# First norm of a two-block layer: x turned raw into place, the root spread by TensorE, two units fed tile by tile

## What is computed

```python
def rms_norm(x, w):
    xf = x.astype(jnp.float32)
    y = xf * lax.rsqrt(jnp.mean(xf * xf, axis=-1, keepdims=True) + RMS_EPS)
    return (y * w.astype(jnp.float32)).astype(x.dtype)

h = rms_norm(x, norm_mix[i])
proj = h @ w_in          # 3*1024 columns q, k, v, 1024 z, then 8 b and 8 a (the gates)
beta = jax.nn.sigmoid(b)
g = -jnp.exp(a_log) * jax.nn.softplus(a + dt_bias)
...
x = x + y                # raw x is needed again after the mixer
```

## Time and profile before

| | |
|---|---|
| median of 3 executions | 1184.47 us |
| the profiled execution | 1184.73 us |
| its span | 1182.8 us |
| TensorE busy | 1120.5 us (95%) |
| VectorE, ScalarE, GpSimd busy | 591.1, 468.8, 486.8 us |
| DMA | 100.36 MB, 85 GB/s on average |

### The profile page before, as it was taken

One profiled execution on the slowest core, in us unless ns is written; L12 is line 12 of the kernel. 1 busy time (PEld: TensorE's weight loads), 2 busy tenths in 40 slices (PEclk: granted clock), 3 DMA queues, 4 the chain that ended last, 5 costly groups with the idle time before them and its releaser, 6 DMA issues. The chain is left out here.

```text
span 1182.8 us, 16417 instructions
## 1 busy us (share of the span) xinstructions
PE 1120.5 (95%) x5820; PEld 908.8 (77%) x5820; DVE 591.1 (50%) x1246; ACT 468.8 (40%) x1002; POOL 486.8 (41%) x280
## 2 busy tenths in 40 slices
PE   5998989999999899999999999989999999999995
PEld 4887778888887787887888888867788887656674
DVE  3696835556655564632122125445754654344465
ACT  5544235555544342342232243243334434343343
POOL 4576312223225495585475475445121211123230
PEclk9999999999999899999999999989999999999998
DMA  7443332211112432632642643503102020001011
GB/s 218 124 111 98 108 83 67 63 46 48 52 36 73 151 111 86 196 122 75 195 133 62 196 144 106 156 20 87 47 26 81 1 63 19 19 9 37 19 37 71
DMA packets 161174, 100.36 MB, mean 85 GB/s; under 512 B 24064, under 2 KB 154444, under 8 KB 160076
## 3 DMA queue, kind: packets, MB, share of 16 engines
q1 hardware_dynamic: 160812, 98.80, 28.7%
q10 hardware_dynamic: 288, 0.59, 0.1%
HBM read 96.21 MB, written 3.16 MB: 84 GB/s over the span
## 5 line engine op out<-in xcount | busy, mean ns | idle before, releaser
L1160 POOL TENSOR_TENSOR wlo<-stage,whi 128x1024 fp32r<-128x1024 f32 (+1 forms) x105 | 272.5, 2599 | 261.9 <-ACT whi L705 261.8
L2092 PE MATMUL ps<-hhi,whi 128*128 128x512 f32 (+1 forms) x744 | 308.2, 414 | 13.8 <-DVE zs L1445 5.5
L2092 PE MATMUL ps<-hlo,whi 128*128 128x512 f32 (+1 forms) x744 | 303.8, 408 | 0.0
L2092 PE MATMUL ps<-hhi,wlo 128*128 128x512 f32 (+1 forms) x744 | 296.8, 399 | 0.0
L2092 PEld LDWEIGHTS ps<-hhi,whi 128*128 128x128 f32 (+1 forms) x744 | 142.1, 191 | 57.6 <-issue 17.1
L2092 PEld LDWEIGHTS ps<-hhi,wlo 128*128 128x128 f32 (+1 forms) x744 | 142.0, 191 | 25.7
L705 ACT ACTIVATE whi<-stage 128x1024 fp32r<-128x1024 f32 x104 | 109.5, 1055 | 130.8 <-PE ps L2092 99.8
L2092 PEld LDWEIGHTS ps<-hlo,whi 128*128 128x128 f32 (+1 forms) x744 | 142.3, 191 | 24.5 <-issue 3.1
L1249 POOL TENSOR_TENSOR wlo<-stage,whi 128x1024 fp32r<-128x1024 f32 (+3 forms) x40 | 73.4, 1838 | 197.3 <-ACT whi L990 197.3
L2092 PE MATMUL ps<-ahi,whi 128*128 128x512 f32 x320 | 127.6, 399 | 5.0 <-POOL alo L1237 3.3
L1066 ACT ACTIVATE prob<-ps,aneg 128x128 f32<-128x128 f32 (+1 forms) x96 | 50.6, 527 | 201.4 <-issue 103.8
(11 more groups left out here) (365 smaller groups left out, 1804.5 us busy)
## 6 DMA issues: line engine op xcount, KB each, us to landing
stage<-dn_w_in SPq DMA_DIRECT2D x32, 512.0 KB, 4.0
stage<-mlp_w_up SPq DMA_DIRECT2D x32, 512.0 KB, 4.5
stage<-mlp_w_down SPq DMA_DIRECT2D x32, 512.0 KB, 4.6
mod_w<-ada_w SPq DMA_DIRECT2D x8, 1536.0 KB, 6.5
stage<-w_in SPq DMA_DIRECT2D x17, 512.0 KB, 3.6
gcrow<-gc_rows SPq DMA_DIRECT2D x16, 256.0 KB, 3.3
stage<-dn_w_out SPq DMA_DIRECT2D x8, 512.0 KB, 3.6
stage<-w_in SPq DMA_DIRECT2D x9, 256.0 KB, 3.1
```

What stands on the lines that cost most here:

```text
L1160: pool.tensor_tensor(wlo[:, slot, 0:ks, 0:cols], stage[:, slot, 0:ks, 0:cols], whi[:, slot, 0:ks, 0:cols], ALU.subtract).then_inc(s["w_lo" ...
L2092: mm = pe.matmul(bank, w[:, slot, k - ks[0], 0:width], x[:, k], start=(i == 0), stop=(i == len(todo) - 1))
```

## The change

The gain is loaded as 8 rows of 128 (4 KB) and turned by TensorE into a column `gcol`. TensorE turns raw x of each token tile as soon as it has landed, in two PSUM banks, and VectorE copies 1024 columns at once into `xT`, its place for later. The reciprocal root of a token tile becomes a diagonal matrix (`tensor_scalar` of the identity), and a product of ones by that diagonal gives a row of roots on all partitions (`ps` bank 1), copied to `rsrow` by ScalarE. Then VectorE makes eight normed tiles `hf0` from `xT`, `gcol` and `rsrow`, all in SBUF, where x had been; ScalarE copies each to `hhi`. The low parts are made by VectorE (even tiles, after all eight) and GpSimd (odd tiles, between its second and third weight split). TensorE feeds the gate unit and the first key unit together: all of high by high, tile by tile as they come; then low weights by high; then high weights by low. The key weights' high part is now made ahead of the tiles. The raw turns and their copies between the later units are gone. The squares of ScalarE go to `hlo` rather than PSUM.

```diff
@@ -320,8 +320,12 @@
-        gbc = sb("gbc", [P, D])
-        xr = sb("xr", [P, 2, D])
+        rsrow = sb("rsrow", [P, T])
+        diag = sb("diag", [P, CH, P])
+        ones0 = sb("ones0", [P, P])
+        nmix = sb("nmix", [P, P])
+        gcol = sb("gcol", [P, KT])
+        hf0 = at("hf0", [P, KT, T], F32, act_at)
...
@@ -705,21 +709,22 @@
...
-            act.dma_start(gbc[:, :], A["norm_mix"].broadcast_to([P, D])).then_inc(s["gbc_in"], 16)
+            act.dma_start(nmix[0:KT, :], A["norm_mix"][0].rearrange("(k p) -> k p", p=P)).then_inc(s["nm_in"], 16)
...
-                act.activation(ps[:, 6:8, :], xn[:, c, :].rearrange("p (b n) -> p b n", b=2), ACT.Square,
+                act.activation(hlo[:, KT - 2:KT, :], xn[:, c, :].rearrange("p (b n) -> p b n", b=2), ACT.Square,
                                scale=float(D) ** -0.5, accum_out=msq[:, c:c + 1]).then_inc(s["x_sq"], 1)
...
-            for f in range(2 * CH):
-                c, half = f // 2, f % 2
-                act.wait_ge(s["h_tr"], f + 1)
...
-            for n in range(1, 4):
+            act.wait_ge(s["rs_ps"], CH)
+            act.activation(rsrow[:, :], ps[:, 1, :], ACT.Copy).then_inc(s["rs_ev"], 1)
+            split_hi(1, 1)
+            for k in range(KT):
+                act.wait_ge(s["x_f"], k + 1)
+                act.activation(hhi[:, k], hf0[:, k], ACT.Copy).then_inc(s["h_hi"], 1)
+            for n in range(2, 4):
                 split_hi(n, n)
...
@@ -781,10 +786,6 @@
...
-                if h == 1:
-                    for k in range(6, KT):
-                        act.wait_ge(s["xtr"], k + 1)
-                        act.activation(xT[:, k], ps[:, (2, 3, 6, 7)[k - 4], :], ACT.Copy).then_inc(s["xev_a"], 1)
...
@@ -1161,6 +1162,7 @@
...
+            pool.memset(ones0[:, :], 1.0).then_inc(s["ones_set"], 1)
...
@@ -1170,8 +1172,13 @@
...
             pool.tensor_copy(whi[:, 0, :, 0:BA_N], stage[:, 0, :, 0:BA_N]).then_inc(s["ba_hi"], 1)
-            for n in range(4):
-                split_lo(n, n, BA_N if n == 0 else P)
+            split_lo(0, 0, BA_N)
+            split_lo(1, 1)
+            for k in range(1, KT, 2):
+                pool.wait_ge(s["h_hi"], k + 1)
+                pool.tensor_tensor(hlo[:, k], hf0[:, k], hhi[:, k], ALU.subtract).then_inc(s["h_lo_p"], 1)
+            for n in range(2, 4):
+                split_lo(n, n)
...
@@ -1327,30 +1334,26 @@
...
-            def x_normed(c):
-                if c >= 2:
-                    dve.wait_ge(s["h_tr"], (c - 1) * 2)
...
+            dve.wait_ge(s["nm_tr"], 1)
+            dve.tensor_copy(gcol[:, :], ps[:, 0, 0:KT]).then_inc(s["nm_col"], 1)
+            for c in range(CH):
                 dve.wait_ge(s["x_rms"], c + 1)
                 dve.reciprocal(rtok[:, 1, c:c + 1], rtok[:, 0, c:c + 1]).then_inc(s["x_inv"], 1)
                 dve.wait_ge(s["x_inv"], c + 1)
-                dve.scalar_tensor_tensor(out=xr[:, c % 2], in0=xn[:, c, :], scalar=rtok[:, 1, c:c + 1], in1=gbc[:, :],
-                                         op0=ALU.mult, op1=ALU.mult).then_inc(s["x_nrm"], 1)
+                dve.tensor_scalar(diag[:, c, :], K["ident"], rtok[:, 1, c:c + 1], None, ALU.mult).then_inc(s["x_dg"], 1)
+                b = 2 + c % 3 * 2
+                dve.wait_ge(s["xtr"], c + 1)
+                dve.tensor_copy(xT[:, :, c * P:(c + 1) * P], ps[:, b:b + 2, :].rearrange("p b (k i) -> p (b k) i", k=KT // 2))\
+                    .then_inc(s["xev"], 1)
+            dve.wait_ge(s["nm_col"], 1)
+            dve.wait_ge(s["xev"], CH)
+            dve.wait_ge(s["rs_ev"], 1)
+            for k in range(KT):
+                dve.scalar_tensor_tensor(out=hf0[:, k], in0=xT[:, k], scalar=gcol[:, k:k + 1], in1=rsrow[:, :],
+                                         op0=ALU.mult, op1=ALU.mult).then_inc(s["x_f"], 1)
+            for k in range(0, KT, 2):
+                dve.wait_ge(s["h_hi"], k + 1)
+                dve.tensor_tensor(hlo[:, k], hf0[:, k], hhi[:, k], ALU.subtract).then_inc(s["h_lo"], 1)
...
@@ -1422,9 +1425,6 @@
...
-            for k in range(6):
-                dve.wait_ge(s["xtr"], k + 1)
-                dve.tensor_copy(xT[:, k], ps[:, (2, 3, 6, 7)[k % 4], :]).then_inc(s["xev_d"], 1)
...
@@ -2100,43 +2100,60 @@
...
-            for f in range(2 * CH):
-                c, half = f // 2, f % 2
...
+            pe.wait_ge(s["nm_in"], 16)
+            pe.transpose(ps[:, 0, 0:KT], nmix[0:KT, :], ident[0:KT, 0:KT]).then_inc(s["nm_tr"], 1)
+
+            def raw_turn(c):
+                pe.wait_ge(x_in[c], 16)
+                if c >= 3:
+                    pe.wait_ge(s["xev"], c - 2)
+                for k in range(KT):
+                    mm = pe.transpose(ps[:, 2 + c % 3 * 2 + k // 4, k % 4 * P:(k % 4 + 1) * P], xn[:, c, k * P:(k + 1) * P], ident)
                 mm.then_inc(s["xtr"], 1)
+
+            def root_row(c):
+                pe.wait_ge(s["x_dg"], c + 1)
+                pe.matmul(ps[:, 1, c * P:(c + 1) * P], ones0[:, :], diag[:, c, :], start=True, stop=True).then_inc(s["rs_ps"], 1)
+
+            pe.wait_ge(s["ones_set"], 1)
+            raw_turn(0)
+            for c in range(1, CH):
+                raw_turn(c)
+                root_row(c - 1)
+            root_row(CH - 1)
...
-            unit(0, 0, hhi, hlo, BA_N, ready=lambda k: pe.wait_ge(s["h_lo"], 7 + k // 4))
+            pe.wait_ge(s["ba_hi"], 1)
+            pe.wait_ge(s["w_hi"], 1)
+            first = ((0, BA_N, ps[0:BA_N, 0, :]), (1, P, ps[:, 1, :]))
+            for k in range(KT):
+                pe.wait_ge(s["h_hi"], k + 1)
+                for n, width, bank in first:
+                    pe.matmul(bank, whi[:, n, k, 0:width], hhi[:, k], start=(k == 0), stop=False)
             pe.wait_ge(s["vec_in"], 16 * (len(VEC_ROWS) + 4))
-            pe.wait_ge(s["x_sq"], CH)
             pe.transpose(ps[:, 7, 0:NVEC], rows[0:NVEC, 0, :], ident[0:NVEC, 0:NVEC])
             pe.transpose(ps[:, 7, P:P + 96], rows[0:96, 1, :], ident[0:96, 0:96]).then_inc(s["vec_tr"], 1)
-            stream = unit_parts(1, 1, hhi, hlo)
...
+            for n, width, bank in first:
+                pe.wait_ge(s["w_lo"], n + 1)
+                for k in range(KT):
+                    pe.matmul(bank, wlo[:, n, k, 0:width], hhi[:, k], start=False, stop=False)
+            for k in range(KT):
+                if k % 2:
+                    pe.wait_ge(s["h_lo_p"], k // 2 + 1)
+                else:
+                    pe.wait_ge(s["h_lo"], k // 2 + 1)
+                for n, width, bank in first:
+                    mm = pe.matmul(bank, whi[:, n, k, 0:width], hlo[:, k], start=False, stop=(k == KT - 1))
+                    if k == KT - 1:
+                        mm.then_inc(s["w_used"], 1)
...
-            some(stream, 24)
-            pe.wait_ge(s["vec_col"], 2)
-            for k in range(4):
-                raw_turn(k)
...
@@ -2183,9 +2200,6 @@
...
-            for k in range(4, KT):
-                raw_turn(k)
-            pe.wait_ge(s["xev_a"], 2)
...
```

31 lines of the change are left out of this document (1 added, 30 removed).

## The result

Twenty executions of the changed kernel have a median of 1186.61 us (1185.27 to 1190.28), beside 1184.46 (1183.20 to 1186.61) for twenty of the kernel before: ratio 1.0019, 95% interval 1.0011 to 1.0027. In a second series, twelve and 24 executions, it was 1186.98 against 1184.98, ratio 1.0022 [1.0012, 1.0032]. The change costs 2.0 to 2.15 us. Forecast were 1187.9, 3.4 more than before, and slower.

A forecast was written before the change was run, and what follows sets the result against it. TensorE was taken as nearly full from 47.60 us on, so only the head counted: -5.0, +7.2, +2.4, +1.4 and -2.6 net +3.4, put on the median 1184.47 for 1187.9 us. Own range 1186.8 to 1191.5.

The forecast's parts named there:

- Start of matrix work, -5.0: TensorE's first joint pass: starts at 16.3 us instead of 21.27, 5.0 earlier.
- The normed tiles: VectorE's eight multiplications alternate with GpSimd's split and low parts, ending at 26.3; eighth high tile at 27.0, 20.9 without contention.
- The joint stage, +7.2: Gate and first key units with their turns take 21.0 us instead of 13.8, both ending at 37.3.
- the mark: Start of the third key unit, by which the change is judged: forecast at 51.0 us, 3.4 later than 47.60.
- The course of the clock: TensorE's clock in the joint passes: slow until near 31 to 32, after unbroken work from 27.0 or 28.3.
- The gate chain, +2.4: From both units' end to the second key unit: 4.7 us instead of 2.3, the chain being waited for uncovered.
- Second key unit, +1.4: Its 24 matmuls after TensorE's idling: 7.15 us instead of 5.75, the clock penalty taken as 1.4 (0 to 2.9).
- The shift is carried to the end: After the third key unit's start: its shift of 3.4 us reaches the kernel's end one for one.
- rival 1: Head of the kernel: same mechanism, cheaper by 0.7 to 2.9 us through an earlier or high clock; 1186.1 us, chance 0.17.
- Rival 2: Normed tiles: GpSimd gets little of the port until VectorE's queue is empty; 1183.1 us, chance 0.10.
- rival 3: Normed tiles: VectorE and GpSimd don't hold each other up; third key unit at 42.5, 1179.4 us, chance 0.17.
- rival 4: Joint pass: held by a late load (gain row or key weights), not fed by tiles; over 1191.5 us, chance 0.03.

The follow-up runs named there:

- root_psum: Changed kernel with the row of roots left in PSUM, ScalarE's copy of it gone, raw turns on two pairs of banks: 1180.85 us, ratio 0.9968 against before.
- after: The changed kernel itself, without further edits: median 1186.61 us, in a second series 1186.98.
- gate_first: Changed kernel with the gate unit finished alone, its turns between two passes of the first key unit: 1184.14 us, ratio 0.9996 against before.
- root_gate: Changed kernel with roots left in PSUM and the gate unit's low products and turns ahead of the first key unit's: 1181.24 us, ratio 0.9970 against before.
- first profile: First profiled execution of the unedited changed kernel, one of the quick ones among its twenty: 1185.37 us.
- second profile: Another profiled execution of the unedited changed kernel, from its second series, standing for the median: 1186.95 us.
- filler12: Changed kernel with 12 unused identity multiplications in TensorE's wait for the gate logs: 1186.56 us, ratio 1.0013 against before.
- k1_cover: Changed kernel with gate sums behind the second key unit's first twelve matmuls, their turn behind its last: 1189.15 us, ratio 1.0033 against before.
- root_gate_hold: root_gate with GpSimd's later weight splits held until VectorE's four low tiles are made, gate turns amid the key unit's last pass: 1178.78 us, ratio 0.9947.

## Why the prediction was right, and where it was off

**Direction and mechanism: right.** Slower by 2.0 to 2.15 us where 3.4 was forecast, by the two things named: multiplications that wait for GpSimd, and a gate chain with nothing beside it. Each was shown by removal: 5.8 us for the first (root_psum against after), 2.5 for the second (gate_first). The two prices don't add up: both removals together (root_gate) bring 5.4 to 5.9 us. They outweigh what the change gains, the earlier start of matrix work and the raw turns that are gone.

**Start of matrix work, -5.0: right.** 16.21 (16.3). ScalarE squares the fourth tile of x from 8.91 (9.2), and the first weights are there at 10.16 (10.4). The third and fourth diagonal took 1.02 and 0.92 us beside GpSimd's cast and split, the first two 0.29 each while GpSimd was idle.

**The normed tiles: right in kind, 1.1 us too dear in both profiles.** Eight end at 25.2 (26.3), the last high tile at 25.9 (27.0). I had added a split and three low parts in full, 6.05 us; the comparison with root_psum gives 5.2. GpSimd waited 1.29 us twice for high tiles ([1.29 <-ACT hhi L726]), in which VectorE went on alone. The low parts of GpSimd are 1.7 us and not 1.29.

**The joint stage, +7.2: mis-sized, +4.4 in the first profile and +6.0 in the second.** Both units end at 34.4 or 35.9 (37.3), and that is the whole difference in the mark, 48.18 or 49.65 for 51.0. It has two parts. The pass over the low weights starts at 26.87 or 26.73 instead of 28.3: 1.1 to 1.2 us of this are the tiles above, and 0.35 the last pair of matmuls and the turns of vectors, for which the clock was up already. In the second profile, the one that stands for the median, that is nearly all: from there to the last pass it takes 5.33 us (26.73 to 32.06), and the forecast had 5.3. In the first it takes 3.73 (26.87 to 30.60), 1.6 less, and this part is the clock's.

**The course of the clock: wrong in both profiles.** I let it rise at 31 to 32. It rose at 25.65 in one, at 23.6 in the other, there with a fall from 27.0 to 30.4. TensorE had worked with pauses of 0.5 to 1.3 us (in the other profile up to 1.6) since 16.2, busy 7.30 of 10.15 us, and the clock rose all the same; I had assumed from the kernel before, where the rows are unbroken, that it would wait for such rows. That the forecast's 5.3 us for the pass fits the second profile is luck: a rise and a second fall gave the same sum as one late rise. My lower bound of 35.8 for the end of both units was too high for the first profile.

**The gate chain, +2.4: right.** 34.43 to 39.20 is 4.77 us (4.7).

**Second key unit, +1.4: right.** 39.20 to 46.48 is 7.28 us (7.15) for 5.75, and 7.25 in the second profile, by a low clock of 3.4 us in both. filler12 shows that the idle time makes it. The size was taken from one wait of the kernel before; another wait there, 3.03 us long, is followed by no slow stretch, so that part of this hit is luck.

**kT is not the bound: right.** It is there at 45.1, ahead of 46.5; in the runs where the unit got faster it became the bound at once (k1_cover, filler12).

**The shift is carried to the end: right for this kernel.** From mark to end 1135.2 us before, 1135.3 and 1135.5 after. It isn't right for every edit: 1139.2 in k1_cover, 1136.9 in root_gate_hold, 1136.5 in gate_first, but 1134.3 in root_psum. New waits for squares (0.57 us in gate_first) and other stretches of low clock stand behind these marks; how much each takes is not shown.

**Rivals.** The median, 1186.61 us, lies 0.2 us below my forecast's own range of 1186.8 to 1191.5, between its 1187.9 and the 1186.1 of rival 1 (the same mechanism, cheaper). Half of that rival's condition came true: the clock rose earlier, but the second unit wasn't fast. The second profile has its mark, 49.65 within 48.6 to 49.9, but there the earlier rise gave hardly anything and the cheaper tiles did; the first profile, where the rise did give something, has its mark below that range. Rival 2 is refuted by GpSimd's low tiles from 18.25 on, in the middle of the multiplications; rival 3 by 10.56 us against 5.36; had it held, the result would have been root_psum's or better, and its price of 1179.4 was near root_psum's 1180.85. Of rival 4 nothing shows: the pass waits for tiles, not for a load.

## What to carry to other kernels

Before VectorE is given work with two inputs in SBUF beside GpSimd work that reads SBUF, be it other tiles, price their instructions as a sum, not side by side, or put one operand in PSUM; and after curing one such place look at the next line, where the hold-up may turn up again. When two units are merged so that both end together, whatever hung on the first loses its cover: order their last passes so that the one with followers ends first. An idle time of about 3 us on TensorE ahead of full work costs its own length and can cost a slow stretch behind it (3.4 or 6.8 us here, and none at 118.25 in the kernel before). So a wait can be worth filling, which has to be tried, and where it is moved to matters as much as its length.
